# Sixteen gate products of each DeltaNet chunk moved from the chunk's end into the three levels of the inverse

## The reference

```python
h = rms_norm(x, norm_mix_w)
proj = h @ w_in                 # q, k, v, z, alpha, beta, FoX parts, merge gates mga, mgb
(gq, gk, gv, gz, ga, gb, fq, fk, fv, ff, fo, mga, mgb) = split(proj)

# chunked delta rule, per head
lower = where(strict, einsum('cd,sd->cs', kb, k) * decay, 0)
sol = triangular_solve(lower + eye(c), concat([vb, kb * exp(gc)]))
u, w = sol[:, :dv], sol[:, dv:]
v_new = u - w @ state
o = (q * exp(gc)) @ state + qk @ v_new
state = state * exp(g_last) + k_dec.T @ v_new
```

## Time and profile before

| | |
|---|---|
| median of 3 runs | 1266.75 us (1264.16 to 1267.02) |
| profiled execution | 1267.03 us |
| its span, first to last instruction | 1265.3 us |
| mean granted TensorE clock | 0.980 |
| busy: PE, DVE, ACT, POOL | 96%, 42%, 34%, 37% |
| DeltaNet stage in the trace | about 176 to 480 us, some 75.5 us per chunk |

### The profile page before, as it was taken

How to read it: one execution, slowest core, us unless ns; L and a number is a source line. 1 busy time by engine, 2 the same in 40 slices (tenths; PEclk the granted TensorE clock), 3 DMA queues, 4 the chain that set the end, 5 groups by cost and what they waited for, 6 DMA issues and landing times.

```text
span 1265.3 us, 16872 instructions
## 1 busy us (share of the span) xinstructions
PE 1218.7 (96%) x6213; PEld 1014.0 (80%) x6213; DVE 529.6 (42%) x1003; ACT 431.3 (34%) x680; POOL 467.2 (37%) x228
## 2 busy tenths in 40 slices
PE   5999979999999999999999998999999999999997
PEld 4868868889888887888888877888788888888886
DVE  4334445362534632666666654542333333340001
ACT  4344442433324233434334433223333322231222
POOL 5334432240423323233223323443444444443443
PEclk8999989898999989999999999999999999999999
DMA  6223321130212214222333216442233333332231
GB/s 172 81 71 93 92 65 51 59 92 26 84 48 80 65 56 128 84 82 84 91 91 91 91 51 199 133 120 81 85 97 99 99 99 90 93 100 84 100 117 67
DMA packets 169630, 113.58 MB, mean 90 GB/s; under 512 B 6257, under 2 KB 157922, under 8 KB 169586
## 3 DMA queue, kind: packets, MB, share of 16 engines
q1 hardware_dynamic: 163218, 98.26, 26.8%
q10 hardware_dynamic: 6368, 14.72, 3.2%
HBM read 104.54 MB, written 8.42 MB: 89 GB/s over the span
## 4 chain that ended last, share of the span: by engine, by line
PE 64%; issue 19%; DVE 7%; POOL 6%; ACT 1%; SPq 1%; DMA 0%; DVEq 0%; POOLq 0%; ACTq 0%
PE ps L1280 43%; PE ps L1655 9%; PE ps L1344 8%; POOL w_lo L545 6%; PE ps L1262 2%; DVE prod L1043 1%; DVE Wb L1046 1%; DVE Lc L1021 1%; PE ps L1591 1%; DVE tmp L927 1%; POOL osc L540 1%; DVE Zm L1050 0%; DMA raw<-in_w_in 0%; ACT w_hi L616 0%; PE ps L1333 0%
## 5 line engine op out<-in xcount | busy, mean ns | idle before, releaser
L545 POOL TENSOR_TENSOR w_lo<-raw,w_hi 128x1024 fp32r<-128x1024 f32 x170 | 419.3, 2467 | 763.2 <-ACT w_hi L616 739.9
L1280 PE MATMUL ps<-h_hi,w_lo 128*128 128x512 f32 x992 | 407.7, 411 | 0.0
L1280 PE MATMUL ps<-h_hi,w_hi 128*128 128x512 f32 x992 | 392.4, 396 | 2.5 <-ACT gate L699 1.7
L1280 PE MATMUL ps<-h_lo,w_hi 128*128 128x512 f32 x992 | 390.5, 394 | 0.0
L616 ACT ACTIVATE w_hi<-raw 128x1024 fp32r<-128x1024 f32 x170 | 180.0, 1060 | 600.4 <-PE ps L1280 507.2
L1280 PEld LDWEIGHTS ps<-h_lo,w_hi 128*128 128x128 f32 x992 | 187.5, 189 | 39.0 <-issue 0.4
L1280 PEld LDWEIGHTS ps<-h_hi,w_hi 128*128 128x128 f32 x992 | 188.4, 190 | 36.1 <-issue 2.3
L1280 PEld LDWEIGHTS ps<-h_hi,w_lo 128*128 128x128 f32 x992 | 188.7, 190 | 32.8 <-issue 1.0
L927 DVE SCALAR_TENSOR_TENSOR tmp<-ps,prm,tmp 128x511 f32<-128x511 f32 (+2 forms) x72 | 53.9, 749 | 92.0 <-ACT tmp L646 86.9
L1218 DVE TENSOR_TENSOR f_lo<-tmp,f_hi 128x512 f32 (+1 forms) x22 | 39.1, 1775 | 35.1 <-ACT f_hi L839 35.1
L893 DVE TENSOR_SCALAR ms<-ss 128x1 f32<-128x1 f32 x8 | 1.2, 154 | 124.2 <-ACT raw L866 117.4
(11 more groups left out here) (234 smaller groups left out, 1594.3 us busy)
## 6 DMA issues: line engine op xcount, KB each, us to landing
raw<-in_w_in SPq DMA_DIRECT2D x80, 512.0 KB, 3.8
raw<-in_w_gate SPq DMA_DIRECT2D x22, 512.0 KB, 3.7
raw<-in_w_up SPq DMA_DIRECT2D x22, 512.0 KB, 3.7
raw<-in_w_down SPq DMA_DIRECT2D x22, 512.0 KB, 3.2
gate_dram<-gate ACTq DMA_DIRECT2D x24, 256.0 KB, 2.0
cumb<-cum_dram ACTq DMA_DIRECT2D x8, 512.0 KB, 3.5
raw<-in_w_branch_a SPq DMA_DIRECT2D x8, 512.0 KB, 4.6
raw<-in_w_branch_b SPq DMA_DIRECT2D x8, 512.0 KB, 3.7
```

The lines of the kernel that those rows point to most:

```text
L545: pool.tensor_tensor(w_lo[:, r % 2, :], raw[:, r, :], w_hi[:, r % 2, :], ALU.subtract)\
L1280: return pe.matmul(ps[:, bank, :], wts[wl][k], acts[xl][:, k, :], start=(n == 0), stop=(n == len(PASSES) - 1))
```

## The change

Twelve products leave the long fill behind the next chunk's decay (30 to 18), and four leave the remainder at the chunk's end (19 to 15). Sixteen come into the inverse: the four fills of levels 0 and 1 have 6 in place of 3, those of the last level 4 and 5 in place of 2 and 3. Nothing else is touched; ACT, POOL, DVE and the DMA queues keep their streams.

```diff
-                    fill(3)
+                    fill(6)
                     for a in range(2):
                         pe.wait_ge(Y_ready, c * 6 + 2 * n + a + 1)
                         pe.wait_ge(T_ready, c * 6 + 2 * n + a + 1)
                         per_head(a, lambda h, m: mm(half_bank(a)[:, h, :], Tm[:, m, :], Yn[:, m, 0:C // 2]), Zd_done)
-                    fill(3)
+                    fill(6)
...
                 for a in range(2):
                     per_head(a, lambda h, n: mm(half_bank(2 + a)[:, h, :], L[64:P, n, :], Zm[64:P, n, 64:P]),
                              Y_done)
-                fill(2)
+                fill(4)
                 for a in range(2):
                     pe.wait_ge(T_ready, c * 6 + 4 + a + 1)
                     pe.wait_ge(Y_ready, c * 6 + 4 + a + 1)
                     per_head(a, lambda h, n: mm(half_bank(4 + a)[:, h, :], Tm[0:64, n, :], Yn[0:64, n, 0:C // 2]),
                              Zd_done)
-                fill(3)
+                fill(5)
...
                 if c < TT - 1:
                     pe.wait_ge(o_ready, led(o_ready, c * 2 + 2))
                     decay(c + 1)
-                fill(30)
+                fill(18)
                 pe.wait_ge(of_ready, led(of_ready, c + 1))
```

## The result

The change makes the kernel slower: 1307.82 us in the median (1304.27 to 1308.54, 4 runs) against 1265.86 us; ratio 1.0327, 95% interval 1.0311 to 1.0342, some 41 us. The forecast was 1288, with 1300 as its upper end. The profiled execution took 1307.5 us with a span of 1305.8 us, 40.5 us more than the span before. The mean granted clock went from 0.980 to 0.966.

The account below looks back on a forecast made before the run. PE, busy for 96% of the span, bounds the kernel, losing time only in waits and at half rate. +23.8 us at full clock, less 3.6 for the clock, made +20.2 on 1267.03 us; forecast 1288, range 1277 to 1300.

Parts of the forecast that it names:

- The wait for unit 4: Last fill of the inverse: PE stands for unit 4's low half on POOL, 3.5 us per chunk, all on the path.
- the wait for unit 5: Long fill: the tenth product waits for unit 5's low half, 2.6 us in chunks 0 to 2.
- The products' price: Inverse: one product costs 0.228 us at full clock, sixteen more cost 3.65 us per chunk.
- No wait for unit 3: Index 72, unit 3: no wait, as POOL did it and then idled 20.42 us before unit 4's low half.
- the +23.8 us of the sum: Whole kernel at full clock: +6.24 per chunk, four chunks +25.0, less 1.2 for chunk 3.
- What the long fill gives back: Long fill: nothing in chunks 0 to 2, the twelve products (2.74 us) turn into 2.7 us of wait.
- my gain of 1.2 us: Chunk 3's end: no decay there, so the chain to the output starts up to 1.2 us earlier, once.
- The clock: Half-rate stretch, one fall per chunk: costs 2.5 us in place of 3.4, minus 3.6 us in all.
- a second fall at the end: Rival, chunk's end: a second clock fall costs 2.4 us per chunk, total 1297 to 1300; chance 0.15.
- the relief: Wait for unit 4: 1 to 3 us of the 6.8 us half-rate stretch lie in it, saving 0.9 us per chunk.
- rival 1: Inverse: sixteen wide products keep the clock at 2.4 GHz and the wait doesn't lower it; +10.2, 1277; chance 0.12.
- the third rival: Chunk's end: PE stands, issues nine products, stands again, and the clock falls a second time; 1297 to 1300; chance 0.15.

Follow-up runs that it names:

- the mends: Against the changed kernel: ScalarE's early work on unit 2 and unit 4's high half, and GpSimd waiting for the scaled output; both together 1267.46 us.
- early_copy_of_unit_2: Changed kernel with ScalarE's work on unit 2 and on unit 4's high half put behind its Tm copies of level 1; 1279.84 us, ratio 1.0117.
- unit4_wait_alone: Kernel before, with PE made to wait for unit 4's low half ahead of the inverse's last fill's third product, no product moved; 1280.80 us, ratio 1.0117.
- levels_0_1_only: Against the kernel before, only the twelve products of levels 0 and 1 moved, taken from the long fill; 1292.56 us, ratio 1.0217.
- last_level_only: Against the kernel before, only the four products of the last level moved, taken from the long fill (26); 1269.14 us, ratio 1.0029.
- gpsimd_waits_for_output: Changed kernel with GpSimd starting the low half of the next chunk's unit 0 only after VectorE wrote the scaled output; 1289.98 us, ratio 1.0197.
- last_level_and_gpsimd_wait: Against the kernel before, only the last level's four products moved, plus GpSimd waiting for the scaled output; 1258.67 us, ratio 0.9945.
- both_mended: Changed kernel with ScalarE's early work on unit 2 and unit 4's high half, and GpSimd waiting for the scaled output; 1267.46 us, ratio 1.0011.

## Why the prediction was wrong

**Right.** The wait for unit 4 (forecast 3.5, measured 3.3 us in each chunk; added alone 3.2 per chunk). The nine products, the wait for unit 5 (2.6 forecast, 2.41 in the bracket), and that the long fill gives nothing back. The products' price: 0.228 us each. No wait for unit 3, none in levels 0 and 1. At full clock this is the +23.8 us of the sum.

**The step that failed first** stands under "What the long fill gives back": "two DVE steps, transposes at 325.16 as before". I took the chain from the decay as fixed and didn't ask what ACT and POOL do earlier once unit 4 ends before the long fill. The high half of the next unit moves up, POOL has its low half ready to start behind `osc`, and DVE's `osc` is held for 2.1 us more: 8.4 us in four chunks. In chunk 3 my gain of 1.2 us was there (L1090 is held for 1.01 us and not for 2.34, as unit 5's low half comes earlier), but under the same loss: 9.48 us against 8.70. The 3.41 us of the mask on E and the 2.34 us of L1090, in the trace of before, would have told it.

**The second, and by its size the larger,** is the clock, under "The clock": I took 3.6 us off for it. In the three stretches of the table the half-rate time outside PE's waits rose from 27.3 to 51.1 us in the trace's clock record, which costs half of the difference, 11.9 us. I took one fall per chunk, cheaper by 0.9 us for lying partly in the wait, and priced a second fall at the end as a rival with 0.15. That rival came true in all four chunks; the falls in the row products I did not have at all (4.4 us between the row products and the first `Zm` transpose); and the relief was not there. By stretch: in rows to decay 31.1 us against 14.6 for products and 13.2 for the wait (the `Zm` waits gave 2.0 back); between the transposes and the next chunk +0.2 instead of −2.7; and behind the last transposes +2.8 instead of −0.9. The upper end, 1300, was the sum for two falls without the held `osc`.

**"The clock is held" (rival 1)** gets its answer from the mends: in the six versions that have four more products in the last level and no wait for unit 4, that level and all behind it up to the decay run at 2.4 GHz in every chunk, 24 of 24. In the changed kernel the wait for unit 4 undoes that. early_copy_of_unit_2 shows it: the wait was worth 28 us with its consequences, not 14.

**The rule beside the sum.** The changed kernel has half-rate stretches at both of its new waits: in each chunk the clock falls while PE waits for unit 4, and again behind the wait of 2.4 us for unit 5 (chunks 0 to 2) or in the wait of 3.4 us for the output (chunk 3). The Trainium skill (page "TensorE: Matmul & The Clock Gate", section "Why this matters for your kernels") advises against idle gaps between bursts of matmuls, as they bring the half rate back, and that was a better guide here than my relief. But it speaks of gaps longer than the 2.4 us wait, so my step from it to the third rival read more into it than it says. And it doesn't cover the stretches with no idle ahead of them.

**Not settled:** what in narrow products makes the clock fall in the row products or in the last level, and what decides in which executions it does. The runs show that richer fills in the last level went with a clock that held, that a wait in a half-rate stretch went with a longer one (unit4_wait_alone), and that the row products fell in some executions and not in others: with `osc` held in three chunks (levels_0_1_only) or one (last_level_only), without it in none (gpsimd_waits_for_output), two (last_level_and_gpsimd_wait) or three (both_mended). So it isn't shown either that the falls in the row products of the changed kernel come from the change, though they cost it time.

## What to carry to other kernels

When work is moved, list what is now *finished* earlier and follow every engine that reacts: here a unit that ended early let GpSimd start a 2.4 us instruction beside a 0.17 us one of VectorE, and PE waited for that. A product that needs prepared operands can only be moved as far forward as the preparing engines' own order allows; move their steps first. And a wait on PE can cost more than its length, through the clock and through the other engines: the changed kernel lost 42 us, of which the two mends of waits, each of a few lines, returned 40.

## What the hardware showed that I had not expected

- A VectorE instruction on 128x8 elements with two SBUF inputs took 2.31 us when it started beside GpSimd's `w_lo` and 0.17 us without it; one on 128x1024 elements 3.41 and 1.22 us. Where VectorE's started first (gpsimd_waits_for_output), GpSimd's `w_lo` took 3.30 us in place of 2.35.
- The granted clock fell with PE never idle, in products of 64 rows and 64 columns and in the narrow row products, and the same instructions ran at full clock in other executions, also with nothing edited ahead of them.
- A standstill of 3.3 us in a half-rate stretch went with one of 10.2 us in place of 6.8, in all four chunks of unit4_wait_alone.
- With 4 and 5 wide products among the small ones of the last level, and no wait for unit 4, the clock stayed at 2.4 GHz from there to the decay in all 24 cases (six versions). With 2 and 3, and no wait for unit 4, it fell there in 16 of 20 (five versions).
